# Second mixer: one product for both directions of a level, weight remainders on GpSimd, rotation on VectorE, block copies on ScalarE

## The reference, cut to what matters

```python
log_f = log(lb + (1 - lb) * sigmoid(z))      # z: forward gate, and backward gate reversed
k_in  = (1 - lb) * sigmoid(-z)
# chunks of 64: o = (q * exp(cumsum(log_f))) @ state + masked(q k exp(differences of the cumsum)) @ v
```

## Time and profile before

| what | us |
|---|---|
| median of 3 runs | 968.34 (966.61 to 1050.31) |
| the profiled execution | 969.81 |
| its span | 968.0 |
| PE busy in the span | 928.2 (96%) |
| DVE busy | 595.9 (62%) |
| ACT busy | 508.5 (53%) |
| POOL busy | 119.0 (12%) |

### The profile page before, as it was taken

How to read it: one execution, slowest core, us unless ns; L and a number is a source line. 1 busy time by engine, 2 the same in 40 slices (tenths; PEclk the granted TensorE clock), 3 DMA queues, 4 the chain that set the end, 5 groups by cost and what they waited for, 6 DMA issues and landing times.

```text
span 968.0 us, 13656 instructions
## 1 busy us (share of the span) xinstructions
PE 928.2 (96%) x4579; PEld 764.9 (79%) x4579; DVE 595.9 (62%) x885; ACT 508.5 (53%) x733; POOL 119.0 (12%) x107
## 2 busy tenths in 40 slices
PE   7999999999999899999999999799899999999986
PEld 5788888888787677888888778689777888888775
DVE  5655455568756546555555566888756666666654
ACT  6544444465745545544444475333536667666553
POOL 5210000020133202000000011432202000000020
PEclk9999999999999999999999999999999999999999
DMA  9796667447622234656655537332245665565511
GB/s 311 211 270 199 203 199 220 137 138 237 214 67 87 66 97 134 212 189 190 185 186 185 184 102 247 109 101 74 66 130 173 196 195 187 173 193 174 175 44 44
DMA packets 122040, 157.43 MB, mean 163 GB/s; under 512 B 10047, under 2 KB 83011, under 8 KB 122000
## 3 DMA queue, kind: packets, MB, share of 16 engines
q1 hardware_dynamic: 119648, 151.65, 49.2%
q0 software_dynamic: 1904, 4.65, 1.9%
q10 hardware_dynamic: 448, 0.59, 0.2%
HBM read 155.79 MB, written 1.07 MB: 162 GB/s over the span
## 4 chain that ended last, share of the span: by engine, by line
PE 85%; DVE 6%; ACT 4%; issue 2%; POOL 1%; SPq 1%; DMA 1%; DVEq 0%; ACTq 0%; POOLq 0%
PE bank L467 25%; PE bank L469 24%; PE bank L468 24%; PE bank L567 2%; DVE w_lo L1542 2%; PE bank L968 2%; ACT w_hi L1103 1%; PE bank L625 1%; PE bank L795 1%; PE bank L793 1%; PE bank L803 1%; SPq L372 1%; DMA w_raw<-in_w_ffn_up 1%; ACT junk L1126 1%; PE bank L937 0%
## 5 line engine op out<-in xcount | busy, mean ns | idle before, releaser
L467 PE MATMUL bank<-w_hi,x_hi 128*128 128x512 f32 (+1 forms) x848 | 340.3, 401 | 10.3 <-DVE hb L1603 2.8
L1549 DVE TENSOR_TENSOR w_lo<-w_raw,w_hi 128x1024 fp32r<-128x1024 f32 x180 | 220.5, 1225 | 181.0 <-ACT w_hi L1112 180.1
L469 PE MATMUL bank<-w_hi,x_lo 128*128 128x512 f32 (+1 forms) x848 | 331.1, 390 | 0.0
L468 PE MATMUL bank<-w_lo,x_hi 128*128 128x512 f32 (+1 forms) x848 | 330.4, 390 | 0.0
L1112 ACT ACTIVATE w_hi<-w_raw 128x1024 fp32r<-128x1024 f32 x180 | 190.6, 1059 | 178.4 <-PE bank L469 178.4
L467 PEld LDWEIGHTS bank<-w_hi,x_hi 128*128 128x128 f32 x848 | 160.1, 189 | 51.8 <-issue 12.3
L469 PEld LDWEIGHTS bank<-w_hi,x_lo 128*128 128x128 f32 x848 | 160.1, 189 | 34.2
L468 PEld LDWEIGHTS bank<-w_lo,x_hi 128*128 128x128 f32 x848 | 160.5, 189 | 29.8
L1542 DVE TENSOR_TENSOR w_lo<-w_raw,w_hi 128x1024 fp32r<-128x1024 f32 x97 | 120.3, 1266 | 50.1 <-ACT w_hi L1103 49.5
L1103 ACT ACTIVATE w_hi<-w_raw 128x1024 fp32r<-128x1024 f32 x108 | 112.1, 1055 | 54.5 <-PE bank L469 50.6
L467 PE MATMUL bank<-w_hi,h_hi 128*128 128x512 f32 (+1 forms) x304 | 116.6, 384 | 4.2 <-DVE h_lo L1638 1.9
(11 more groups left out here) (278 smaller groups left out, 823.2 us busy)
## 6 DMA issues: line engine op xcount, KB each, us to landing
w_raw<-in_w_ffn_gate SPq DMA_DIRECT2D x132, 256.0 KB, 2.9
w_raw<-in_w_ffn_up SPq DMA_DIRECT2D x132, 256.0 KB, 3.1
w_raw<-in_w_ffn_down SPq DMA_DIRECT2D x132, 256.0 KB, 3.0
w_raw<-in_w_in SPq DMA_DIRECT2D x104, 256.0 KB, 3.1
w_raw<-in_w_out SPq DMA_DIRECT2D x32, 256.0 KB, 3.4
w_raw<-in_w_ple_gate SPq DMA_DIRECT2D x16, 256.0 KB, 3.2
arena<-bias_rows POOLq DMA_DIRECT2D x8, 256.0 KB, 4.5
w_raw<-in_cmp_w_k SPq DMA_DIRECT2D x8, 256.0 KB, 4.9
```

The costliest lines, as they stand in the source:

```text
L467: pe.matmul(out_, hi, wh, start=start, stop=False)
L468: pe.matmul(out_, hi, wl, start=False, stop=False)
L469: return pe.matmul(out_, lo, wh, start=False, stop=stop)
L1549: dve.tensor_tensor(wlo[:, s_], raw[:, s_], whi[:, s_].bitcast(F32), ALU.subtract).then_inc(sem("lo_done"), 1)
```

## The change

The two half products of a level become one: a new buffer KMIX holds, for each block of 2h positions, h keys of one direction beside h keys of the other, made by ScalarE (`key_mix`, 14 copies of 128 x 512), and TensorE multiplies it with the likewise interleaved queries in 4 matmuls of 128 columns. The keys' growth now waits for that copy and no longer for the level's product. The 16 weight remainders of units (p, j) + 6 for p = 4 to 7 move from VectorE to GpSimd, where `grow` and the gating of HGS are put among them. The rotation moves from GpSimd to VectorE, behind `staged2`. The copies of level 0 (`diagonal`) and the copies out of PSUM for groups 6 to 9 of turns (`turned2`) move to ScalarE.

```diff
--- before.py
+++ after.py
@@ -214,6 +214,7 @@
...
 DW = a2.take(512)
+KMIX = (a2.take(512), STG2 + 1024)
@@ -294,9 +295,9 @@
...
-def halves_of(tensor, row, off, h):
-    return raw_ap(tensor, row, off, [[2 * h, 64 // h], [1, h]])
+def both_ways(off, n, h):
+    return raw_ap(arena, ARENA, off, [[2 * h, n // (2 * h)], [1024 + h, 2], [1, h]])
@@ -333,16 +334,19 @@
...
-PL0, PL1 = U_QA[1] + RING, U_OUT1 + 6
+POOL_UNITS = ((U_QA[1] + RING, U_OUT1 + 6), (U_IN2 + 16 + RING, U_OUT2 + 6))
+def pool_before(u):
+    return sum(min(max(u - a, 0), b - a) for a, b in POOL_UNITS)
...
-    if PL0 < u <= PL1:
-        return sem("lo_pool"), u - PL0
-    return sem("lo_done"), u if u <= PL0 else u - (PL1 - PL0)
+    if any(a < u <= b for a, b in POOL_UNITS):
+        return sem("lo_pool"), pool_before(u)
+    return sem("lo_done"), u - pool_before(u)
 def lo_shift(base):
-    return PL1 - PL0 if base >= PL1 else 0
+    return pool_before(base)
@@ -952,11 +956,15 @@
...
             pe.wait_ge(sem("grown_dve"), 2 * (L - 2) + pr + 1)
-            if pr == 1:
+            if L == 8 and pr == 1:
                 pe.wait_ge(sem("grown_pool"), L - 1)
-        if L >= 1:
-            pe.wait_ge(sem("at_done"), n - 1)
+        if 1 <= L <= 7:
+            pe.wait_ge(sem("kmix_done"), n - 1)
+        if L == 1:
+            pe.wait_ge(sem("at0_done"), n - 1)
+        elif L >= 2:
+            pe.wait_ge(sem("at_done"), n - 3)
@@ -964,10 +972,8 @@
...
                     h, c = 1 << (L - 1), (2 * hh + blk) * P
-                    for z, o in ((0, h), (1, 0)):
-                        mm = pe.matmul(halves_of(b, 512, c + o, h), av(HK + 1024 * z + at, [P]),
-                                       halves_of(arena, ARENA, HQ + 1024 * (1 - z) + at + o, h),
-                                       start=True, stop=True)
+                    mm = pe.matmul(b[:, c:c + P], av(KMIX[pr] + hh * S + blk * P, [P]), both_ways(HQ + at, P, h),
+                                   start=True, stop=True)
@@ -1003,7 +1009,8 @@
...
-        pe.wait_ge(sem("at_done"), 18)
+        pe.wait_ge(sem("at0_done"), 2)
+        pe.wait_ge(sem("at_done"), 16)
@@ -1456,14 +1463,50 @@
...
+    def key_mix(n):
+        L, pr = divmod(n, 2)
+        if not 1 <= L <= 7:
+            return
+        if L == 1:
+            act.wait_ge(sem("k_done"), 8)
+            if pr == 1:
+                act.wait_ge(sem("t2_full"), 8)
+        else:
+            act.wait_ge(sem("grown_pool") if pr else sem("grown_k"), L - 1)
+            act.wait_ge(sem("lv_full"), n - 1)
+        h = 1 << (L - 1)
+        act.activation(av(KMIX[pr], [256 // h, 2, h]), both_ways(HK + pr * 512, 512, h), ACT.Copy
+                       ).then_inc(sem("kmix_done"), 1)
+    def diagonal(pr):
+        act.wait_ge(sem("lv_full"), pr + 1)
+        act.activation(raw_ap(arena, ARENA, AT + pr * 1024, [[512, 2], [384, 2], [1, P]]),
+                       bank[4 + pr][:, :].rearrange("p (a b c) -> p a b c", a=2, b=2), ACT.Copy
+                       ).then_inc(sem("at0_done"), 1)
+    def turned2(g):
+        act.wait_ge(sem("t2_full"), g + 1)
+        o = {6: DQT, 7: DQT + 512, 8: DKT, 9: DKT + 512}[g]
+        act.activation(av(o, [512]), bank[2 + g % 2][:, :], ACT.Copy).then_inc(sem(f"t2_done{g % 2}"), 1)
...
         for j in range(4):
+            if (p, j) == (4, 3):
+                diagonal(0)
+                diagonal(1)
+            for n in levels_at(p, j):
+                key_mix(n)
...
             split(U_IN2 + 4 * p + j + RING)
+            if j >= 2 and p in (4, 5):
+                turned2(T2_FIRST[p - 1] + j - 2)
@@ -2103,7 +2146,7 @@
...
         dve.wait_ge(sem("t2_full"), g + 1)
-        o = {0: QT0, 1: QT0 + 512, 6: DQT, 7: DQT + 512, 8: DKT, 9: DKT + 512}[g]
+        o = {0: QT0, 1: QT0 + 512}[g]
@@ -2138,28 +2181,32 @@
...
         b = bank[4 + pr]
-        dve.wait_ge(sem("lv_full"), n + 1)
-        if 1 <= L <= 7:
+        if L == 0:
+            return
+        if L <= 7:
...
                 dve.wait_ge(sem("k_done"), 8)
+            if pr == 0:
+                if L >= 2:
+                    dve.wait_ge(sem("grown_k"), L - 1)
+                dve.wait_ge(sem("kmix_done"), n - 1)
+                dve.tensor_tensor(grown(HK, 0, h), grown(HK, 0, h), growth(0, h, True), ALU.mult
+                                  ).then_inc(sem("grown_k"), 1)
+            dve.wait_ge(sem("lv_full"), n + 1)
...
                 dve.wait_ge(sem("grown_dve"), 2 * (L - 2) + pr + 1)
-                dve.wait_ge(sem("grown_k"), L - 1)
-            if pr == 0:
-                dve.tensor_tensor(grown(HK, 0, h), grown(HK, 0, h), growth(0, h, True), ALU.mult
-                                  ).then_inc(sem("grown_k"), 1)
...
         data = b[:, :].rearrange("p (a b c) -> p a b c", a=2, b=2)
-        if L >= 1:
-            dve.wait_ge(sem("at_done"), n - 1)
-        if L == 0:
-            dve.tensor_copy(raw_ap(arena, ARENA, AT + pr * 1024, [[512, 2], [384, 2], [1, P]]), data
-                            ).then_inc(sem("at_done"), 1)
-        elif L <= 7:
+        dve.wait_ge(sem("lv_full"), n + 1)
+        if L == 1:
+            dve.wait_ge(sem("at0_done"), n - 1)
+        else:
+            dve.wait_ge(sem("at_done"), n - 3)
+        if L <= 7:
@@ -2168,6 +2215,21 @@
...
+    def rotate(n, p):
+        base = STG2 + 1024 * STG2_AT[p]
+        dve.wait_ge(sem("pk_done"), 2 * (p + 1))
+        x1, x2 = (raw_ap(arena, ARENA, base + o, [[512, 2], [HD, 8], [1, 8]]) for o in (0, 8))
+        c, s_ = (raw_ap(small, 512, o, [[8, 2], [0, 8], [1, 8]]) for o in (COS, SIN))
+        r = [av(ROT + 128 * i, [2, 8, 8]) for i in range(4)]
+        if n:
+            dve.wait_ge(sem("rot_done"), 6 * n)
+        for i, (a_, b_) in enumerate(((x1, c), (x2, s_), (x2, c), (x1, s_))):
+            dve.tensor_tensor(r[i], a_, b_, ALU.mult).then_inc(sem("rot_done"), 1)
+        dve.wait_ge(sem("rot_done"), 6 * n + 4)
+        dve.tensor_tensor(x1, r[0], r[1], ALU.subtract).then_inc(sem("rot_done"), 1)
+        dve.tensor_tensor(x2, r[2], r[3], ALU.add).then_inc(sem("rot_done"), 1)
@@ -2246,15 +2308,18 @@
...
                 staged2(p)
+                if p in (3, 4):
+                    rotate(p - 3, p)
...
                 quad_gain(0)
-            split(U_IN2 + 4 * p + j + RING)
-            if j >= 2 and p in (1, 4, 5):
-                turned2(T2_FIRST[p - 1] + j - 2)
+            if p < 4:
+                split(U_IN2 + 4 * p + j + RING)
+            if j >= 2 and p == 1:
+                turned2(j - 2)
@@ -2363,11 +2428,15 @@
...
     lo(1)
-    for u in range(PL0, PL1):
+    def remainder(u):
...
+    for u in range(*POOL_UNITS[0]):
+        remainder(u)
@@ -2382,41 +2451,29 @@
...
-    def rotate(n, p):
-        base = STG2 + 1024 * STG2_AT[p]
-        pool.wait_ge(sem("trig_done"), 2)
-        pool.wait_ge(sem("pk_done"), 2 * (p + 1))
-        x1, x2 = (raw_ap(arena, ARENA, base + o, [[512, 2], [HD, 8], [1, 8]]) for o in (0, 8))
-        c, s_ = (raw_ap(small, 512, o, [[8, 2], [0, 8], [1, 8]]) for o in (COS, SIN))
-        r = [av(ROT + 128 * i, [2, 8, 8]) for i in range(4)]
-        if n:
-            pool.wait_ge(sem("rot_done"), 6 * n)
-        for i, (a_, b_) in enumerate(((x1, c), (x2, s_), (x2, c), (x1, s_))):
-            pool.tensor_tensor(r[i], a_, b_, ALU.mult).then_inc(sem("rot_done"), 1)
-        pool.wait_ge(sem("rot_done"), 6 * n + 4)
-        pool.tensor_tensor(x1, r[0], r[1], ALU.subtract).then_inc(sem("rot_done"), 1)
-        pool.tensor_tensor(x2, r[2], r[3], ALU.add).then_inc(sem("rot_done"), 1)
...
         h = 1 << (L - 1)
-        pool.wait_ge(sem("lv_full"), 2 * L + 2)
+        pool.wait_ge(sem("kmix_done"), 2 * L)
...
                            ).then_inc(sem("grown_pool"), 1)
-    rotate(0, 3)
-    grow(1)
-    rotate(1, 4)
-    for L in range(2, 8):
-        grow(L)
-    pool.wait_ge(sem("vec_in"), 32)
-    for m in range(M):
-        pool.wait_ge(sem("pk_done"), 11 + m)
-        o = av(HGS + 512 * m, [4, P])
-        pool.tensor_tensor(o, o, raw_ap(hb, 1024, 896, [[0, 4], [1, P]]), ALU.mult).then_inc(sem("hgs_done"), 1)
+    for p in range(4, 8):
+        for j in range(4):
+            for n in levels_at(p, j):
+                if n % 2 and 1 <= n // 2 <= 7:
+                    grow(n // 2)
+            remainder(U_IN2 + 4 * p + j + RING)
+            if (p, j) == (7, 0):
+                pool.wait_ge(sem("vec_in"), 32)
+                for m in range(M):
+                    pool.wait_ge(sem("pk_done"), 11 + m)
+                    o = av(HGS + 512 * m, [4, P])
+                    pool.tensor_tensor(o, o, raw_ap(hb, 1024, 896, [[0, 4], [1, P]]), ALU.mult
+                                       ).then_inc(sem("hgs_done"), 1)
```

## The result

The changed kernel takes 974.83 us in the median (974.43 to 980.34, 6 runs) against 968.47 before; the ratio is 1.0071, 95% interval 1.0047 to 1.0096. One run of the kernel before, at 1050.31 us, was slow as a whole and is left out of the ratio. The forecast was 965, so the sign was wrong, though the time lies inside the range. In a later comparison the ratio was 1.005 (1.0026 to 1.0075), 4.4 us in the medians.

A forecast was written before the change was run, and what follows sets the result against it. TensorE, busy 928 of 968 us, was taken as the bound. Terms -12.0 - 7.0 + 5.1 + 3.1 + 1.6 + 3.4 + 0.5 + 2.3 = -3.0 gave 966.8 profiled, 965 us median; 8-in-10 range 951 to 977.

The forecast's parts named there:

- Level products: Levels 1 to 7: 14 products of 16 records become 8 records of 128 columns at 0.112 us each, -12.0 us.
- The product is not cheaper: Rival for the level products: gathered queries stream slower, a record costs 0.183 us, +8, 973 us median; chance 0.04.
- The rotation's wait: Before the transposes of unit (4, 2): TensorE no longer waits for GpSimd's rotation; 2.2 of 9.2 us stay, -7.0 us.
- The port: From 609.8: two-SBUF-operand products on VectorE and GpSimd exclude each other, 15.7 us in a row, T complete about 625.3.
- The kind rival: VectorE holds the port pair through its chain, GpSimd fills holes; 953.6 us, or 952 median; chance 0.20.
- The two stalls: TensorE waits before group 5 for VectorE's half of group 4, +5.1 us, and before level 4 for operands, +3.1 us.
- The clock behind level 4: After the second stall TensorE runs about 3.2 us at half rate: +1.6 us (0 to 1.6).
- Pairs of levels: Groups 5 and 6: two stalls behind the exponentials, +3.4 us (2.2 to 5.6), and query waits elsewhere, +0.5 (0 to 1).
- The chain exponentials to mix: In (6, 0) and (6, 2) ScalarE does exponentials before the next key mixes: two stalls of at least 1.1 us, taken as 1.7.
- The tail: Group 7: GpSimd remainders of (7, 2) and (7, 3) can hold VectorE's last attention weights and gating, +2.3 us (0 to 4.6).
- Slower: remainders in every pair: Rival, groups 6 and 7: a remainder delays second queries at each of four pairs, +14 with clock, 976 us median; chance 0.15.
- about +6 with all high ends: Upper end of the forecast sum's own range, all waits at their high ends; the kind end was -16 us.

The follow-up runs named there:

- experiment 1: All 16 moved remainders back on VectorE, against the changed kernel: 961.3 us, ratio 0.9935 to the kernel before; stretch 102.8 us.
- experiment 7: Only the rotation moved to VectorE, against the kernel before: 971.4 us, ratio 1.0049; stretch 110.4 us.

## Why the prediction was wrong, point by point

**Level products, right but for the first levels.** From h = 4 on a record costs 0.112 from one start to the next, as forecast, and gathered queries cost nothing. With h = 2 (levels 4 and 5) it is 0.120, and with h = 1 (levels 2 and 3), where the queries come from the other place after every element, 0.166, in every kernel with the fused product and at full clock. That is 1.0 us that the -12.0 lacks, and for one pair nearly the rival "The product is not cheaper" (0.183).

**The rotation's wait, right.** From the transposes of (4, 2) to the next unit 2.5 us (619.73 to 622.23), forecast 2.2.

**The port, right as a mechanism.** T was forecast to end at 625.3 (609.8 + 15.7 is 625.5, a slip of 0.2); it ends at 629.6 less 6.15, 623.5. From HQ's start to T's end are 13.9 us (615.66 to 629.61), where the sum had 15.7. The kind rival is excluded: GpSimd stepped into every gap of the chain for which it had an instruction ready, with KSUM behind HQ and with the three remainders behind the first three T products. The two stalls were forecast at 5.1 and 3.1 and came out at 2.0 and 3.4; TensorE itself was 1.4 later there than I had it (628.3 less 6.15 against 620.8), of which 0.9 are the dear records of levels 2 and 3. Level 4 began at 636.72, which is 630.6 in the times of before: forecast 631.8, before 632.39. What it waited for last was not its queries but the masked copy of level 2, which frees the bank and which the chain of the forecast left out. Up to there the account held within 1.2 us, with errors of both signs.

**The clock behind level 4, too low.** +1.6 (0 to 1.6) was forecast. Level 4's product and the next unit took 6.27 us (636.72 to 642.99), at a granted clock of 0.50; with the remainders on VectorE (experiment 1) and full clock the same two took 3.8. So it was +2.5, outside its own range.

**Pairs of levels, too low: the first of the two steps that turned the sign.** I gave the waits in groups 5 and 6 3.4 + 0.5 and their clock nothing. They are 3.2, 0.2, 0.7 and 3.3 (levels 10, the first turn, 12, 14), and behind the last one the product of 16 records takes 3.21 us (680.29 to 683.50) instead of 1.87, at half clock. At the start of the last scores TensorE is at 699.74, which is 693.59 in the times of before, against 693.27: +0.3, where the sum had -5.3. Of these 5.6 us, 3.5 are the waits (7.4 where 3.9 stood), 1.3 the clock behind level 14 and 0.9 the clock behind level 4, less 1.2 by which level 4 began sooner; about 1 us more lies in gaps inside products and units that are too short for the list of waits. The waits have two causes, by the experiments. The chain exponentials to mix, forecast at 1.1 at the least, measures 0.8 with short remainders; the rest of 3.2 and 3.3 is port time of the queries. The bound "one remainder adds up to 1.7" had VectorE's first queries before the remainder and only the second behind it. In the trace the queries ahead of level 10 take 1.48 and 2.26 instead of 0.68 each, the first held by GpSimd's key growth and the second by a remainder, 2.4 more in sum; ahead of level 14 it is the first that a remainder holds, 2.85, and the second takes 0.67: 2.2 more.

**The tail, too low: the second of the two.** +2.3 (0 to 4.6) was forecast, the middle of the range. The stretch's remaining part grew by 5.7, and taking two remainders away gave 5.8 back. Both instructions of the attention weights were held, 5.09 us for 0.88, and the clock behind them, which the sum left out, comes on top. I had taken the middle because start times decided it, and saw no reason for either end. There was one: `split` on ScalarE ends about when the weights begin, since both are released by the same exponentials, so they met in all four traces of kernels that have these two remainders whole on GpSimd, with a wait of 5.9 in each.

**The rivals.** "Slower: remainders in every pair" had mechanism and place right, and its +14 for four pairs was too much (the four pairs came to 8.7 with the clock), but it got 0.15. The true case lies between it and the forecast, with the tail on top: -3.0 + 5.6 (up to the last scores) + 3.4 (tail) = +6.0, as measured. That my "about +6 with all high ends" gives the same number is luck: the two first stalls came out 2.8 below the forecast, and clock that stood in no term made up for it. I left the high ends of two waits that one cause, the port, sets together as if they were independent, and took the middle of each.

## What to carry to other kernels

Before moving an elementwise operation of two tensors between VectorE and GpSimd, add both engines' two-tensor work in the stretch as if one engine did it, and look for a short dependent chain on VectorE: here each of its gaps admitted one GpSimd instruction of full length. A move that frees the bounding engine pays only if the next thing it meets is ready too: look up what that is before the move. When several waits hang on one cause, don't take the middle of each as if they were independent. And where an operand is gathered from two places, price the finest pattern by itself.

## What the runs showed of the hardware

GpSimd's TENSOR_SCALAR with **one** tensor input did not hold VectorE's two-tensor products, its TENSOR_TENSOR with **two** did: 16 instructions of 2.1 us of the first kind left L2256 at 0.74 us, 16 of 2.6 of the second made it 1.21. The Trainium skill says in "SBUF — State Buffer" (section "SBUF: two separate sides") that such a VectorE op contends with a GpSimd op that reads SBUF. These runs agree for two tensor inputs and not for one; the measurement decides. Second, a record of 128 columns whose moving operand changes between two places after every element cost 0.166 us at full clock, after every two 0.120, and in runs of four or more 0.112. Third, how long TensorE ran at the lower clock does not follow from the length of the wait: 3.2 us before level 10 left the clock at 1.00, 3.4 before level 4 brought 0.50 until about 642, 3.3 before level 14 brought 0.50 until about 683, and 2.5 in experiment 7 brought 0.50 for the ten us from 625 to 635.
